# Indexer scores of a hybrid decoder trunk: from VectorE to ScalarE and GpSimd, with the token shifts cut in parts

## The reference, cut to what matters

```
# sparse attention, for each query block of 128 tokens, 8 indexer heads h
logits = einsum('bqhd,bsd->bqhs', iq, ik) * 64**-0.5
score  = einsum('bqhs,bqh->bqs', relu(logits), iw)     # sum over heads of relu(logit) * weight
score  = where(key <= query, score, -inf)
sel    = top_k(score, 256)                             # then softmax attention over sel only
# RWKV inputs: zb + (token_shift(zb) - zb) * mu
# pooling inputs: trailing-window means (2, 4, 8, 16) minus the token
```

## Time and profile before

| what | value |
|---|---|
| median of 3 runs | 4057.21 us (4056.69 to 4059.38) |
| profiled execution | 4065.51 us, of which 4063.7 us are the span of the trace |
| busy in the span | PE 90%, DVE 46%, POOL 24%, ACT 23% |
| mean granted PE clock | 0.908 of full speed |
| the six steps, layer 1 | 177.4 to 727.6 us |
| the six steps, layer 2 | 2174.5 to 2724.5 us |

### The profile page before, as it was taken

The page is one execution under the profiler, slowest core; times in us unless marked ns, Lnnn a source line. Parts: engine busy times, 40 slices in busy tenths (PEclk is TensorE's granted clock), DMA queues, the critical chain, the costliest instruction groups (busy, mean ns, idle before and its releaser), DMA issues.

```text
span 4063.7 us, 60832 instructions
## 1 busy us (share of the span) xinstructions
PE 3667.1 (90%) x23288; PEld 2636.0 (65%) x23288; DVE 1864.7 (46%) x3137; ACT 950.9 (23%) x1681; POOL 978.4 (24%) x844
## 2 busy tenths in 40 slices
PE   7889888798899999999988898877989999999997
PEld 3444445488657888888734444456867578888884
DVE  4388887443351222222326888864442512222224
ACT  2121211344221222111121112114431212112222
POOL 1042222154211222222100421232632112222221
PEclk9877886699899999999997888857999999999998
DMA  3100000000111111111010000000001111111110
GB/s 112 33 12 11 16 11 11 17 1 1 32 47 37 47 46 47 51 46 50 33 43 24 16 11 16 16 6 13 0 1 45 38 47 47 49 44 52 46 46 42
DMA packets 38005, 128.27 MB, mean 32 GB/s; under 512 B 7264, under 2 KB 7776, under 8 KB 36960
## 3 DMA queue, kind: packets, MB, share of 16 engines
q1 hardware_dynamic: 37568, 125.29, 9.5%
q10 hardware_dynamic: 288, 1.05, 0.1%
HBM read 120.04 MB, written 5.24 MB: 31 GB/s over the span
## 4 chain that ended last, share of the span: by engine, by line
PE 56%; issue 30%; POOLq 6%; DVE 2%; POOL 2%; ACT 1%; DVEq 1%; DMA 1%; ACTq 0%; SPq 0%
PE bank L982 13%; PE bank L983 13%; PE bank L984 13%; PE bank L707 3%; PE wide L575 2%; PE wide L580 1%; PE bank L652 1%; PE wide L707 1%; PE bank L675 1%; PE wide L638 1%; POOLq L1416 1%; PE bank L871 1%; POOLq L1286 1%; POOLq L1327 1%; PE bank L930 1%
## 5 line engine op out<-in xcount | busy, mean ns | idle before, releaser
L1415 POOL TENSOR_TENSOR WL<-WR,WH 128x1024 fp32r<-128x1024 f32 x160 | 388.8, 2430 | 1496.6 <-ACT WH L1229 1495.9
L605 PE MATMUL bank<-X,WR 128*128 128x512 f32 x1152 | 568.3, 651 | 20.9 <-ACT X L1043 9.9
L982 PE MATMUL bank<-XH,WH 128*128 128x512 f32 x1280 | 517.5, 404 | 19.5 <-DVE XL L1461 10.0
L984 PE MATMUL bank<-XH,WL 128*128 128x512 f32 x1280 | 501.6, 392 | 0.0
L983 PE MATMUL bank<-XL,WH 128*128 128x512 f32 x1280 | 501.6, 392 | 0.0
L605 PEld LDWEIGHTS bank<-X,WR 128*128 128x128 f32 x1152 | 236.8, 211 | 327.4 <-issue 296.5
L1801 DVE TENSOR_TENSOR Y<-Y,bank 128x512 f32<-128x512 f32 x256 | 176.0, 687 | 491.9 <-PE bank L984 491.9
L982 PE MATMUL bank<-HH,WH 128*128 128x512 f32 x1024 | 400.3, 391 | 0.0
L983 PE MATMUL bank<-HL,WH 128*128 128x512 f32 x1024 | 398.7, 389 | 0.0
L984 PE MATMUL bank<-HH,WL 128*128 128x512 f32 x1024 | 398.5, 389 | 0.0
L1788 DVE TENSOR_TENSOR RB<-RB 128x512 f32<-128x512 f32 x128 | 88.6, 692 | 561.3 <-ACT RB L1255 561.3
(11 more groups left out here) (265 smaller groups left out, 5342.9 us busy)
## 6 DMA issues: line engine op xcount, KB each, us to landing
WR<-in_w SPq DMA_DIRECT2D x128, 512.0 KB, 3.5
WR<-in_w_in SPq DMA_DIRECT2D x36, 512.0 KB, 3.5
WR<-in_w_out SPq DMA_DIRECT2D x16, 512.0 KB, 3.5
WR<-in_w_gate SPq DMA_DIRECT2D x16, 512.0 KB, 5.9
Y<-in_xT SPq DMA_DIRECT2D x2, 2048.0 KB, 13.5
out_T<-X SPq DMA_DIRECT2D x1, 4096.0 KB, 11.1
UQ<-in_w_uq SPq DMA_DIRECT2D x2, 1024.0 KB, 7.4
PE_IN<-in_pT SPq DMA_DIRECT2D x2, 1024.0 KB, 4.9
```

What stands on the lines that cost most here:

```text
L605: mm = e.matmul(BK_[hf], WR[:, i % RING, kt, :], X[:, kt, hs(hf)], start=kt == 0, stop=kt == KT - 1)
L982: e.matmul(BK_[b], WH[:, s, w, :], high[:, kt, q], start=kt == 0, stop=False)
L984: mm = e.matmul(BK_[b], WL[:, s, w, :], high[:, kt, q], start=False, stop=kt == kts - 1)
L1415: e.tensor_tensor(WL[:, s, :, :], WR[:, i % RING, :, :], WH[:, s, :, :].bitcast(F32), ALU.subtract)
```

## The change

On ACT, the relu of a head is followed by a drain and a second activation, a copy with the query's weight as scale. For head 0 it writes straight into `SC`, for heads 1 to 7 back into `R`. POOL then adds `R` to `SC` for heads 1 to 7 and adds the causal mask after head 7. DVE has no `lg` work left; it waits for `scores_ready` ahead of a block's first round. ACT's relu of head h now waits for POOL's add of head h - 2 (heads 0 and 1 for the block before). ACT also takes over the wait for `bias_ready` ahead of head 0. New semaphores carry these waits, and the two counts that `relu_used` started with are dropped.

The shifts, which stood in one piece behind each `bias` item, are cut into 6 parts of one or two instructions (the two pooling blocks into 2 halves) and spread by columns over the items of the next b. In POOL's queue that gives, for b = 4: two of the four pooling halves and the adds in the order half, add 1, 2, 3, half, add 4, 5, half, add 6, 7, half, `bias`; in the later steps there are 12 to 18 short parts among the seven adds.

```
@@ -133,6 +133,14 @@
     return out + extra[k:]
 
 
+SHIFT_PARTS = 6
+
+
+def shift_parts(tiles):
+
+    return [("shift", i, part) for i in tiles for part in (range(2) if i in (PZ0, PZ1) else range(SHIFT_PARTS))]
+
+
 def mix_plan():
 
 
@@ -146,7 +154,7 @@
     at = 10
     plan += [z[7], ("vt", 0, 0)] + spread_in(attention_items(0, first), z[8:at])
     plan += [("vt", 1, 0), ("iq", second, 0), ("q", 1, 0)]
-    shifted = 5
+    shifted, waiting = 5, []
 
     def whole_blocks():
         return [i for i in range(ZW) if ("z", i, 1) in z[:at]]
@@ -162,11 +170,12 @@
             items.append(("iq", after[after[b]], 0))
         items.append(("q", b, 0))
         rounds = [("round", b, i) for i in range(ROUNDS)]
-        plan += items[:1] + rounds[:HEAD_START] + spread_in(items[1:], rounds[HEAD_START:])
+        items = items[:1] + rounds[:HEAD_START] + spread_in(items[1:], rounds[HEAD_START:])
+        plan += spread_in(items, shift_parts(waiting))
         plan.append(("bias", b, 0))
-        plan += [("shift", i, 0) for i in range(shifted, len(whole_blocks()))]
+        waiting = range(shifted, len(whole_blocks()))
         shifted = len(whole_blocks())
-    plan += z[at:] + attention_items(last) + [("shift", i, 0) for i in range(shifted, ZW)] + [("rms", 0, 0)]
+    plan += z[at:] + attention_items(last) + shift_parts([*waiting, *range(shifted, ZW)]) + [("rms", 0, 0)]
     return plan
 
 
...
+        weights_ready, weighted = sem("weights_ready"), sem("weighted")
         NTOP = NB - FIRST_TOPK
         N_BIAS = NB - 1
 
...
@@ -1149,8 +1158,22 @@
                     elif kind == "lg":
                         n, w = (b + 1) * P, h % 2
                         e.wait_ge(wide[w].full, wide[w].written(L, ("lg", b, h)))
-                        e.wait_ge(relu_used, L * (NTOP * IH) + (TOP_ORDER.index(b) * IH + h + 1))
+                        k = TOP_ORDER.index(b) * (IH - 1)
+                        if h > 2:
+                            e.wait_ge(relu_used, L * (NTOP * (IH - 1)) + (k + h - 2))
+                        elif h < 2 and k:
+                            e.wait_ge(relu_used, L * (NTOP * (IH - 1)) + (k - 1 + h))
                         e.activation(R[:, w, 0:n], WIDE[w][:, 0:n], ACT.Relu).then_inc(wide[w].free, 1)
+                        if h == 0:
+                            e.wait_ge(weights_ready, L * 2 + (1 + b // (NB // 2)))
+                            if ATT_AT[b] >= 4:
+                                e.wait_ge(bias_ready, L * N_BIAS + (ATT_AT[b] - 1))
+                            settle(e)
+                        e.drain()
+                        to = R[:, w, 0:n] if h else SC[:, SLOT[b], 0:n]
+                        e.activation(to, R[:, w, 0:n], ACT.Copy, scale=IW[:, b, h:h + 1]).then_inc(weighted, 1)
+                        if h == 0:
+                            e.drain()
                     elif kind in ("s", "pt"):
                         attention(L, kind, b, h)
                     elif kind == "rms":
@@ -1279,28 +1302,37 @@
             layer_norm(0)
             meet(e, 0, -1)
 
-            def shift(tile, mu):
+            def shift(tile, mu, part):
 
                 d = SHT[:, 0, 0:HALF]
-                e.tensor_tensor(d, tile[:, HALF - 1:S - 1], tile[:, HALF:S], ALU.subtract)
+                if part == 0:
+                    e.tensor_tensor(d, tile[:, HALF - 1:S - 1], tile[:, HALF:S], ALU.subtract)
+                elif part in (1, 4):
+                    e.tensor_scalar(d, d, mu, None, ALU.mult)
+                elif part == 2:
+                    e.tensor_tensor(tile[:, HALF:S], tile[:, HALF:S], d, ALU.add)
+                elif part == 3:
+                    e.tensor_scalar(d[:, 0:1], tile[:, 0:1], -1.0, None, ALU.mult)
+                    e.tensor_tensor(d[:, 1:HALF], tile[:, 0:HALF - 1], tile[:, 1:HALF], ALU.subtract)
+                else:
+                    e.tensor_tensor(tile[:, 0:HALF], tile[:, 0:HALF], d, ALU.add)
                 e.drain()
-                e.tensor_scalar(d, d, mu, None, ALU.mult)
+
+            def scores(L, b, h):
+
+                n, sl, w = (b + 1) * P, SLOT[b], h % 2
+                e.wait_ge(weighted, L * (NTOP * IH) + (TOP_ORDER.index(b) * IH + h + 1))
+                settle(e)
+                e.tensor_tensor(SC[:, sl, 0:n], SC[:, sl, 0:n], R[:, w, 0:n], ALU.add).then_inc(relu_used, 1)
                 e.drain()
-                e.tensor_tensor(tile[:, HALF:S], tile[:, HALF:S], d, ALU.add)
-                e.drain()
-                e.tensor_scalar(d[:, 0:1], tile[:, 0:1], -1.0, None, ALU.mult)
-                e.tensor_tensor(d[:, 1:HALF], tile[:, 0:HALF - 1], tile[:, 1:HALF], ALU.subtract)
-                e.drain()
-                e.tensor_scalar(d, d, mu, None, ALU.mult)
-                e.drain()
-                e.tensor_tensor(tile[:, 0:HALF], tile[:, 0:HALF], d, ALU.add)
-                e.drain()
-
-            def pool(j):
+                if h == IH - 1:
+                    e.tensor_tensor(SC[:, sl, b * P:n], SC[:, sl, b * P:n], causal, ALU.add).then_inc(scores_ready, 1)
+
+            def pool(j, part):
 
 
                 z, n = PZ[:, j, :], POOL_HALO + HALF
-                for hf in (1, 0):
+                for hf in (1 - part,):
                     src, dst = SHT[:, 0, :], SHT[:, 1, :]
                     if hf == 1:
                         e.tensor_tensor(dst[:, 1:n], z[:, S - n + 1:S], z[:, S - n:S - 1], ALU.add)
@@ -1377,7 +1409,7 @@
                 settle(e)
                 e.memset(WK[:, 1, 0:P], 0.0).then_inc(bias_ready, 1)
                 e.tensor_copy(WK[:, 1, P:2 * P], causal).then_inc(bias_ready, 1)
-                for kind, b, _ in plan:
+                for kind, b, part in plan:
                     if kind == "bias" and b != TOP_ORDER[-1]:
                         n, w = (b + 1) * P, SLOT[b]
                         e.wait_ge(topk_done, L * NTOP + (TOP_ORDER.index(b) + 1))
@@ -1385,14 +1417,16 @@
                         e.drain()
                         e.tensor_scalar(WK[:, w, 0:n], WK[:, w, 0:n], 0.0, BIG, ALU.is_equal, ALU.mult)\
                          .then_inc(bias_ready, 1)
-                    elif kind == "shift" and b in B_OF:
-                        for hf in range(2):
-                            e.wait_ge(zbank[hf].free, zbank[hf].read(L, b))
-                        shift(BZ[:, B_OF[b], :], par_col("mu", B_OF[b]))
+                    elif kind == "lg" and part:
+                        scores(L, b, part)
                     elif kind == "shift":
-                        for hf in range(2):
-                            e.wait_ge(zbank[hf].free, zbank[hf].read(L, b))
-                        pool(b - PZ0)
+                        if part == 0:
+                            for hf in range(2):
+                                e.wait_ge(zbank[hf].free, zbank[hf].read(L, b))
+                        if b in B_OF:
+                            shift(BZ[:, B_OF[b], :], par_col("mu", B_OF[b]), part)
+                        else:
+                            pool(b - PZ0, part)
                 meet(e, L, 0)
                 meet(e, L, 1)
                 e.wait_ge(px_ones, L + 1)
@@ -1511,28 +1545,14 @@
                 e.drain()
                 e.tensor_tensor(dst[:, :, :], dst[:, :, :], T2[:, 0:n, :], ALU.add).then_inc(narrow.free, 1)
 
-            def scores(L, b, h):
-
-                n, s, w = (b + 1) * P, SLOT[b], h % 2
-                if h == 0 and ATT_AT[b] >= 4:
-                    e.wait_ge(bias_ready, L * N_BIAS + (ATT_AT[b] - 1))
-                e.wait_ge(wide[w].free, wide[w].read(L, ("lg", b, h)))
-                if h == 0:
-                    e.tensor_scalar(SC[:, s, 0:n], R[:, w, 0:n], IW[:, b, h:h + 1], None, ALU.mult)\
-                     .then_inc(relu_used, 1)
-                else:
-                    e.scalar_tensor_tensor(SC[:, s, 0:n], R[:, w, 0:n], IW[:, b, h:h + 1], SC[:, s, 0:n],
-                                           ALU.mult, ALU.add).then_inc(relu_used, 1)
-                e.drain()
-                if h == IH - 1:
-                    e.tensor_tensor(SC[:, s, b * P:n], SC[:, s, b * P:n], causal, ALU.add)
-                    e.drain()
-
             def topk_round(L, b, i):
 
                 n, s = (b + 1) * P, SLOT[b]
                 work = WK[:, s, 0:n]
                 src = work if i else SC[:, s, 0:n]
+                if i == 0:
+                    e.wait_ge(scores_ready, L * NTOP + (TOP_ORDER.index(b) + 1))
+                    settle(e)
                 e.max(M8[:, :], src)
                 e.drain()
                 e.match_replace(work, M8[:, :], src, BIG)
@@ -1647,10 +1667,8 @@
                         e.tensor_copy(VT[:, k, :], NARROW[0].rearrange("p (k c) -> p k c", k=4)[:, :, 0:72])\
                          .then_inc(narrow.free, 1)
                         e.drain()
-                        e.tensor_scalar(IW[:, k, :], VT[:, k, HD:HD + IH], IH ** -0.5 * HD ** -0.5, None, ALU.mult)
-                        e.drain()
```

(10 more changed lines are left out.)

## The result

The changed kernel takes 4026.4 us at the median of 4 runs against 4057.0 before; the ratio is 0.9925 with a 95% interval of 0.9908 to 0.9942, so 31 us faster (24 to 37). The forecast was 4000. The profiled execution took 4025.1 us with a span of 4023.3. I cut the stage again where the mask of a selected block begins, and ask the windows view of the kernel after, layer 1: head stage, then steps b = 3, 4, 5, 6, 7 and 2. The columns are those of the earlier trace rows.

What follows compares the result with a forecast made beforehand. PE and DVE bound the mixing stage, coupled, neither full. Per layer, 36.7 us step gains less 8.4 rotation and 4.8 head stage, plus 5 clock, make 28.5; 57 for both, 4057.2 to 4000 us, range 3945 to 4048.

Steps and rivals of the forecast that it cites:

- What leaves DVE: Steps b = 3 to 7: DVE is relieved of 65.1 us per layer, 42.4 of it work and 22.7 waits.
- The copies in PE's way: ACT's queue: 5 to 7 copies per step at 0.7 to 1.2 us delay PE 4.9 to 6.0; head stage loses 4.8.
- The smaller of DVE's relief and PE's idle time less the copies: Gain per step, b = 3 to 7: together 36.7 us per layer, 28.3 after 8.4 for PE's waits on the query rotation.
- b = 5: Mixing step b = 5: gain 4.3 us before the rotation's 2.1, 2.2 after it.
- b = 6 and 7: Last two steps with logits, where DVE rules: gains 7.8 (9.9 before the rotation) and 9.7 us.
- The clock's 5 us per layer: PE in the mixing stage: a higher granted clock gives back 5 us per layer, between bounds of nothing and 16.
- a PE that waits less runs faster: Argument for the rival that DVE alone is the bound: PE with fewer waits also gets the higher clock; no separate size.
- POOL and the moved shifts at nothing: POOL's queue: seven adds, 16.5 us per step, and the spread shifts are hidden and cost nothing.
- DVE alone is the bound: Rival for the mixing stage: DVE's relief comes through whole, 75 to 121 us, giving 3937 to 3982; chance 0.25.

Runs made afterwards that it cites:

- kernel without copies: Changed kernel with ACT's scaled copies left out, so the multiplication by the weights is missing and the result is not the reference's: 3963.2 us, ratio 0.9769.
- whole shifts: Changed kernel with POOL's shifts again in one burst behind each mask, as before the change: 4105.7 us, ratio 1.0111 to the kernel before.
- versions with the copies out of PE's way: Changed kernel with scaled copies left out (3963.2 us), queued behind PT's copies (3963.7; 3958.5 with block 3 on DVE), or replaced for heads 1 to 7 by POOL multiplies (3964.2).
- half: Changed kernel with relus of two neighbouring heads back to back on ACT, but the scaled copies still ahead of PT's copies: 4020.7 us, ratio 0.990.
- full deferral: Changed kernel, same instructions, ACT reordered: relus of neighbouring heads back to back, then PT's copies, then the scaled copies: 3963.7 us, ratio 0.9768.

## Why the prediction was right, and where it was off

The direction, the range and the kind of case were right: the copies in PE's way took most of the relief in the early steps, and the late ones gained. The gain was 31 us for 57 forecast, so the size was off by nearly half, and it would have been worse without two errors that went opposite ways: PE's waits gave about a third of what the sum had, its clock about twice. Step by step:

- *What leaves DVE*: right. In b = 3 to 7 DVE is busy for 42.6 us less in layer 1 (407.97 to 365.34), for 42.4 forecast.
- *The copies in PE's way*: right as the time of one copy (0.7 to 1.2 us with its drain). As waits of PE they came to less than priced: in b = 3 and 4 its waits for ACT grew by 4.0 and 3.9 us, for 5.4 and 6.0. The head stage's 10.4 us over both layers for 9.6 agree by luck: 7.3 in one layer and 3.1 in the other, 4.0 of idle time and 6.4 by the clock.
- *The smaller of DVE's relief and PE's idle time less the copies*: this step failed, in b = 3 and 4 above all. It gave 5.2 - 2.1 and 7.6 - 2.1 us, together 17 over both layers, and the steps gave 0.5. PE's idle time of 10.6 and 13.6 us was not all DVE's to give back: 2.7 and 2.5 us of it were waits for ACT's relus already. In b = 3 the wait for maxima went to nothing (4.8 us) and the rotation's fell by 0.9, the waits for ACT rose by 4.0, and PE's busy time rose by 1.7 at a clock of 0.82 for 0.84: nothing is left. In b = 4 maxima and rotation gave 6.1, ACT took 3.9 and the busy time 1.8. The kernel without copies shows the same limit: with nothing in PE's way the two steps gave 6.8 and 7.0 us, not the 8.5 and 11.5 that the slack less the rotation allows. A cost of one engine subtracted from the idle time of another is not a schedule. The 3.1 us forecast for b = 3 are there (3.2) where block 3 stays on DVE and the clock is 0.86, with the same waits.
- *b = 5* gave 7.6 us for 2.2 forecast: here PE's busy time itself fell, from 88.2 to 81.0 us, with the granted clock at 0.87 for 0.81; the idle time gave 0.4.
- *b = 6 and 7* gave 5.9 and 7.2 for 7.8 and 9.7. In b = 6 it was idle time (15.9 to 9.9 us); in b = 7 PE's idle time stayed and its busy time fell by 7.9, while DVE's fell by 6.0.
- *The clock's 5 us per layer* was mis-sized and not a term to add at the end. Over b = 3 to 7 of layer 1 PE's busy time fell by 11.5 us and its idle time by 9.8, where the sum had 5 for the clock and 28.3 for the rest. The clock went up in b = 5 and 7 and down in b = 6 (0.87 to 0.83), though PE's idle time fell there. That a PE that waits less runs faster, as the prediction has it, is not borne out as a rule. With the copies out of the way the clock is 0.83 to 0.92 in b = 3 to 7 instead of 0.77 to 0.88.
- *POOL and the moved shifts at nothing*: right for the kernel as it is, by its order and not by its spare time, as the whole shifts show. The prediction put POOL's busy time at 29.2 us or less in b = 3 to 7; the earlier trace rows has 42.2 in b = 4, and it became 53.2 of 87.4. Of the last passes of the query rotation only that of b = 2 met an add of POOL; it took 1.56 us for 0.56, in both kernels, so the change added nothing there.
- *Rivals*: "DVE alone is the bound" was 3937 to 3982, and the versions with the copies out of PE's way lie in it, at 3958 to 3964. That is its number and not its mechanism: DVE is busy for 54.9 of 67.0 us in b = 3 there, and the gain shows as PE's busy time. What kept the changed kernel from it was the scaled copies' place in ACT's queue.

The Trainium skill's advice to keep elementwise work on VectorE (GPSIMD Engine Reference, "Engine selection") would have been the wrong guide here: POOL's add takes 1.8 times as long as DVE's multiply-add (2.36 to 1.30 us), and a version in which POOL even multiplies is 2.3% faster than the kernel before.

Not settled: by what way the place of PT's copies moves PE's clock. From half to full deferral layer 1's five steps got 32 us shorter, with PE's busy time 36 us down and its idle time 4 us up. No run held the clock fixed, so it isn't shown that the waits at PT's copies lowered it.

## What to carry to other kernels

When work moves to an engine with room, look at what stands behind the new instruction in that engine's queue, not at its busy share: the same 96 copies cost 63 us ahead of PT's copies and nothing that could be measured behind them. A long piece of filler work in the queue of an engine that others wait for must be cut until it fits between two waits, even where it costs nothing today. And a price measured beside the old bottleneck (21 us here) can be far below what it costs once that bottleneck is gone (63 us). When PE's idle time hardly moves and its busy time does, compare the clock of the same rows before looking for waits.

## What I had not expected of the hardware

The granted clock of PE differs between stretches with the same matmuls and the same waits. The head stage of the kernel before took 50.2 us at 0.86 and 53.8 at 0.78, and step b = 3 took 75.0 us at 0.82 in the changed kernel and 72.0 at 0.86 with block 3 on DVE. A stretch of 50 to 75 us can thus move by 3 to 4 us without any change of its own.

The scaled copy took 0.13 us longer than the relu of its shape, 1.15 for 1.02 us at 1024 columns. Two other rows of the kernel after divide that:

```profile
L1187 ACT ACTIVATE A<-wide,PAR 128x1024 f32<-128x1024 f32 x3 | 3.3, 1113 | 6.1 <-PE wide L926 6.1
...
L1195 ACT ACTIVATE BZ<-BZ 64x1024 f32<-64x1024 f32 x1 | 1.1, 1056 | 0.0
```

The first is the same copy with a per-partition scale, but out of PSUM: 1.11 us, 0.10 more than the relu, which has no such operand. The second (another function, on 64 partitions) reads SBUF and has no such operand: 1.06 us, 0.04 more. So most of the 0.13 us goes with the scale operand, and little with reading SBUF. At 384 columns it is the same, 0.62 for 0.48.
